# Layer borders of a hybrid decoder trunk: packed column sums, a smaller root and reciprocal, and loads issued by another queue

## The chip, the cores and the metric

The kernel runs on 1 core of one Trainium2 chip. The metric is the device time of one execution in microseconds, the median of the runs.

## What is computed

A trunk of 4 layers over 1024 prompt tokens and 8 single-token samples, with 1024 features. All is float32. Layers 0 and 3 are of kind a (gated MLP with spatial mixing), layer 1 is of kind b (sliding-window attention with rotary embedding), layer 2 of kind c (a convolution and a gated linear recurrence):

```python
def rms_norm(x, g):
    y = xf * lax.rsqrt(jnp.mean(xf * xf, axis=-1, keepdims=True) + NORM_EPS)
    return (y * g.astype(jnp.float32)).astype(x.dtype)

for i in range(DEPTH):
    hp = rms_norm(xp, norm_pre[i])
    yp = mixer(hp)                       # a, b, c, a; ends in a product with w_out
    xp = xp + rms_norm(yp, norm_post[i])
```

The mean of squares is over the features. So at each border between two layers two norms follow one another: the post norm of the layer that ends (its output must be known for all features of a token) and the pre norm of the layer that begins.

## The kernel before

Tokens lie along the columns (1032 = 3 chunks of 344) and features along the 128 partitions, in 8 tiles (KT). A weight unit is 128 x 1024 values, which make one output tile of 128 features for all tokens. SP loads units into a ring of three (`weights`, L373), ScalarE rounds one to its high part (`w_high`, L848), VectorE subtracts for the low part (`w_low`, L1313), and TensorE adds three products (high by high, high by low, low by high) of 344 columns for each of the 8 feature tiles: 24 products for a chunk, 72 for a unit. Each engine runs its own program, written out by hand; the order in it is fixed, and a wait on a semaphore holds all that stands behind it on that engine or queue.

The border is `cross(prev, L)` on ScalarE and VectorE, `last_pair` and `first_pair` on TensorE. The last two output tiles of a layer are computed chunk by chunk: pieces (0,0), (1,0), (0,1), (1,1), (0,2), (1,2), where the first number is the tile and the second the chunk (L456). `post(L, c)` sums the squares of the outputs over the partitions with two matmuls against a matrix of ones (L490, L491, 128 x 128 by 128 x 344 in plain float32, each two instructions in the trace). The second one reads `rx`, where ScalarE has put the squares of the second tile. ScalarE takes the root of all 344 columns from bank 6 into `rx` (`root_post`, L873), and VectorE its reciprocal (`inverse`, L1341). Then `tiles(c, ks)` runs on VectorE over the 8 feature tiles of the chunk: for two tiles at a time the product with `rx` (L1355), for each the addition to `x` (L1358), and once ScalarE has made the high part `h_hi` (L889) the low part `h_lo` (L1335). ScalarE also squares each new tile of x (L894) into a ring of six, and TensorE sums these squares over the partitions (`square_sum`, L531) between the products of the next layer's first two units (L520). The root of that sum is `root_pre` (L879). The pre norm is applied to the results only, when VectorE reads them (`first_reads`, L1375, and `read`, L1425), which frees their banks. In layers of kind a VectorE must also add the outputs to a first half (`out_add`, L1322) before they are squared.

In `first_pair` the unit 0 of chunk 0 comes first, then unit 1 of chunk 0, then the post sum of chunk 2, then both units of chunk 1 and of chunk 2. The sum of chunk 1 uses bank 6 and waits for the root of the post sum of chunk 2, which stands on ScalarE behind six tiles of chunk 1. Units 2 and 3 follow (`unit_by_parts`). SP stores x after the tiles of each chunk (L397), behind the load of weight 2, so that its place can be used by the layer; weight 3 is issued when the first pair has ended.

Each layer then starts on ScalarE with waits for the stored x and the last low part, and DMAs for its constants: the spatial weights in a (L967 to L971), cosine, sine, mask and sinks in b (L1079 to L1085), the states in c (L1190, L1191). In layer b VectorE waits for all seven loads, then signals that the key is read. ScalarE issues the key's swap of halves for the rotary embedding (four DMAs, L1092), VectorE rotates (L1574 to L1577), ScalarE copies the key (L1100) and issues four output DMAs (L1102 to L1105), and after these the first query's swap. `rotate_q` and the low part of weight 4 stand behind that swap on VectorE. In layer c VectorE computes the decay constants (L1768 to L1791, tiny operations) before the first of eight convolutions (`conv`, L1800 on); the low part of weight 4 stands behind the third.

## Time and profile before

| | us |
|---|---|
| median of 3 runs | 2553.09 (2552.48 to 2553.47) |
| the profiled execution | 2552.86 |
| its span in the trace | 2550.8 |
| TensorE busy | 2382.4 |
| VectorE busy | 1280.9 |
| ScalarE busy | 899.9 |

Times in the rows are microseconds from the span's start unless a row says ns. PE is TensorE, DVE is VectorE, ACT is ScalarE; ACTq and SPq are the queues on which they issue. L12 is line 12 of the kernel. Matmuls are pipelined: the duration of one is about twice the distance to the next. A number in brackets at the end of a row is the idle time before it and what ended it.

### The profile page before, as it was taken

The page shows a single profiled execution, that of the slowest core. Times are in us where ns is not written, and L with a number is a line of the kernel's source. Part 1 is how long each engine was busy: PE and PEld are TensorE (multiplying, and loading weights), DVE is VectorE, ACT ScalarE, POOL GpSimd, SP SyncE. Part 2 cuts the span into 40 slices and gives each one's busy share as a digit, 9 for nine tenths or more (in the row PEclk, how much of TensorE's full clock was granted, in tenths as well). Part 3 has the DMA queues.
Part 4 walks back from the last instruction along what each step waited for, and adds up shares of the span by engine and source line. Part 5 has one row for each costly group of instructions (what it writes and reads, how often), then busy time and mean ns, then how long its engine had stood idle before and what let it go on. Part 6 is the DMA issues. An engine that isn't in the chain of part 4 may idle for free.

```text
span 2550.8 us, 34906 instructions
## 1 busy us (share of the span) xinstructions
PE 2382.4 (93%) x14951; PEld 2295.4 (90%) x14951; DVE 1280.9 (50%) x1769; ACT 899.9 (35%) x1242; POOL 92.9 (4%) x44
## 2 busy tenths in 40 slices
PE   8999999998999869997988989899999999998995
PEld 7998999998999868885988989889998999998995
DVE  4443454545334746665268566456443454545236
ACT  5223223233223325455342356344223323234221
POOL 0000000000000002222000001000000000000000
PEclk9999999999999989998999999999999999999998
DMA  3111111111122421110321111313111111111122
GB/s 128 42 50 42 38 41 47 41 44 34 42 84 65 131 61 51 42 50 26 108 70 58 50 41 34 111 55 95 42 50 34 43 42 44 42 46 35 42 91 93
DMA packets 58490, 145.80 MB, mean 57 GB/s; under 512 B 8904, under 2 KB 29528, under 8 KB 58328
## 3 DMA queue, kind: packets, MB, share of 16 engines
q1 hardware_dynamic: 41936, 116.57, 15.0%
q10 hardware_dynamic: 16400, 27.00, 3.4%
q8 instruction: 118, 1.93, 0.3%
q14 instruction: 36, 0.29, 0.0%
HBM read 121.47 MB, written 18.37 MB: 55 GB/s over the span
## 4 chain that ended last, share of the span: by engine, by line
PE 77%; DVE 10%; ACT 5%; DVEq 2%; DMA 2%; ACTq 2%; issue 1%
PE ps L440 58%; PE ps L664 5%; PE ps L520 3%; PE ps L583 2%; PE ps L531 2%; PE ps L811 1%; DVE w_lo L1313 1%; PE ps L456 1%; PE ps L576 1%; PE ps L706 1%; PE ps L681 1%; DVE x L1358 1%; PE ps L692 1%; DVE l_y_lo L1537 1%; DVE l_acc L1355 1%
## 5 line engine op out<-in xcount | busy, mean ns | idle before, releaser
L440 PE MATMUL ps<-l_h_hi,w_hi 128*128 128x344 f32 x2448 | 529.2, 325 | 39.4 <-DVE w_lo L1313 36.1
L440 PE MATMUL ps<-l_h_lo,w_hi 128*128 128x344 f32 x2448 | 523.0, 322 | 0.0
L440 PE MATMUL ps<-l_h_hi,w_lo 128*128 128x344 f32 x2448 | 519.5, 321 | 0.0
L440 PEld LDWEIGHTS ps<-l_h_hi,w_hi 128*128 128x128 f32 x2448 | 412.3, 190 | 44.0 <-DVE w_lo L1313 38.0
L440 PEld LDWEIGHTS ps<-l_h_lo,w_hi 128*128 128x128 f32 x2448 | 416.8, 190 | 0.0
L440 PEld LDWEIGHTS ps<-l_h_hi,w_lo 128*128 128x128 f32 x2448 | 410.8, 189 | 0.0
L1313 DVE TENSOR_TENSOR w_lo<-w_raw,w_hi 128x1024 fp32r<-128x1024 f32 x182 | 222.6, 1223 | 223.5 <-ACT w_hi L848 203.5
L1425 DVE TENSOR_TENSOR l_tmp<-ps,rx 128x1032 f32<-128x1032 f32 x64 | 78.9, 1233 | 323.9 <-PE ps L440 323.9
L848 ACT ACTIVATE w_hi<-w_raw 128x1024 fp32r<-128x1024 f32 x182 | 190.6, 1047 | 105.7 <-DMA w_raw<-in_wu 65.3
L440 PE MATMUL ps<-l_y_hi,w_hi 128*128 128x344 f32 x912 | 197.5, 325 | 32.4 <-ACT l_y_hi L1036 19.7
L440 PE MATMUL ps<-l_y_hi,w_lo 128*128 128x344 f32 x912 | 193.8, 321 | 0.0
L440 PEld LDWEIGHTS ps<-l_y_hi,w_hi 128*128 128x128 f32 x912 | 154.4, 190 | 36.3 <-issue 16.3
L440 PE MATMUL ps<-l_y_lo,w_hi 128*128 128x344 f32 x804 | 171.9, 322 | 0.0
L440 PEld LDWEIGHTS ps<-l_y_hi,w_lo 128*128 128x128 f32 x912 | 153.3, 189 | 0.0
L992 ACT ACTIVATE l_tmp<-l_tmp 128x1032 f32<-128x1032 f32 x32 | 34.1, 1067 | 304.5 <-DVEq L1466 304.5
L440 PEld LDWEIGHTS ps<-l_y_lo,w_hi 128*128 128x128 f32 x804 | 137.2, 191 | 0.0
L997 ACT ACTIVATE l_tmp<-l_tmp 128x1032 f32<-128x1032 f32 x32 | 34.1, 1067 | 262.8 <-DVEq L1471 262.8
L415 POOL TENSOR_TENSOR l_sc<-l_sc,l_rq 128x1024 f32<-128x1024 f32 x32 | 71.3, 2227 | 1144.5 <-DVE l_rq L1645 1144.5
L976 ACT ACTIVATE l_v<-l_v 128x1032 f32<-128x1032 f32 x32 | 34.1, 1067 | 217.2 <-DVEq L1447 217.2
L1420 DVE TENSOR_TENSOR ssq<-ssq,sqt 128x1032 f32<-128x1032 f32 x50 | 61.7, 1233 | 92.4 <-ACT sqt L959 75.8
L520 PE MATMUL ps<-l_h_hi,w_hi 128*128 128x344 f32 x192 | 89.9, 468 | 9.3 <-DVE w_lo L1313 9.3
L1140 ACT ACTIVATE l_sc<-l_sc,l_mx 128x256 f32<-128x256 f32 x128 | 63.5, 497 | 92.8 <-DVEq L1638 92.8
(242 smaller groups left out, 3617.9 us busy)
## 6 DMA issues: line engine op xcount, KB each, us to landing
w_raw<-in_wu SPq DMA_DIRECT2D x182, 512.0 KB, 3.6
x_save<-x SPq DMA_DIRECT2D x9, 1376.0 KB, 5.5
x<-x_save ACTq DMA_DIRECT2D x24, 516.0 KB, 6.5
x<-in_xt ACTq DMA_DIRECT2D x8, 516.0 KB, 5.8
l_sw<-l_q ACTq DMA_DIRECT2D x32, 129.0 KB, 3.0
out_y<-x SPq DMA_DIRECT2D x6, 688.0 KB, 3.5
x<-in_xt SPq DMA_DIRECT2D x4, 688.0 KB, 10.5
x<-in_xt SPq DMA_DIRECT2D x4, 344.0 KB, 6.2
```

The costliest lines, as they stand in the source:

```text
L415: nc.gpsimd.tensor_tensor(L.sc[:, i % 2], L.sc[:, i % 2], L.rq[:, i % 2].rearrange("p (h o) -> p h o", o=1).to_broadcast([P, 4, 2 * WIN]), ...
L440: mm = nc.tensor.matmul(ps[:, 3 * slot + ch, 0:CW], wt[:, w, k, :], mv[:, k, ch * CW:(ch + 1) * CW], start=(k == 0 and t == 0), stop=(k == ...
L520: mm = nc.tensor.matmul(ps[:, 3 * j + c, 0:CW], wt[:, (u + j) % W_RING, k, :], mv[:, k, part(c)], start=(k == 0 and t == 0), stop=(k == KT ...
L531: mm = nc.tensor.matmul(ps[:, 7 - c % 2, 0:CW], ones[:, :], square_place(c, k), start=(k == 0), stop=(k == KT - 1))
L583: mm = nc.tensor.matmul(ps[:, 6 + b // 4, (b % 4) * P:(b % 4 + 1) * P], vt[:, b, :], L.ws[:, g, :], start=True, stop=True)
L664: mm = nc.tensor.matmul(ps[:, p % 2, 0:CW], wt[:, w % W_RING, k, :], mv[:, k, part(ch)], start=(k == 0 and t == 0), stop=(k == KT - 1 and ...
L848: nc.scalar.activation(w_hi[:, u % W_RING], w_raw[:, u % W_RING], ACT.Copy).then_inc(w_hi_done, 1)
L976: nc.scalar.activation(tile_of(L.v, m), tile_of(L.v, m), ACT.Gelu_apprx_tanh)
L1140: nc.scalar.activation(L.sc[:, p, h, :], L.sc[:, p, h, :], ACT.Exp, bias=L.mx[:, p, 1, h:h + 1], accum_out=L.mx[:, p, 2, h:h + 1])
L1313: V.tensor_tensor(w_lo[:, u % W_RING], w_raw[:, u % W_RING], w_hi[:, u % W_RING], ALU.subtract).then_inc(w_lo_done, 1)
L1420: V.tensor_tensor(total[:], total[:], part, ALU.add)
L1425: V.tensor_tensor(chunks(out), psum_result(slot), chunks(rx[:]), ALU.mult)
```

## The change

Sums over the partitions are made in four groups of 32 output rows. Group g sums columns 86g to 86g + 85 of the chunk, so that the sum of 344 columns stands in 128 partitions by 86 columns (every partition of a group holds the same values). Root and reciprocal work on these 86 columns (`rs`). VectorE then multiplies the 86 columns by a selector `gsel` (1 where the partition is in group g) into 344 columns of `rx`, TensorE multiplies that by the ones (`spread`), which brings each group's values to all partitions, and ScalarE copies the result from the bank to `rx`. The root takes no scale 1/D any more and its bias is 1e-6 D: the spread adds up 32 equal values, and 32 is the root of D = 1024. On TensorE the sums and spreads stand inside pieces (after some k) where the post sum stood behind them. The root of chunk 2 moves ahead of the tiles of chunk 1. The layers' loads go from ScalarE to SP, behind the load of weight 3; the outputs of layer b too. In layer b the signals that key and value are read come first, VectorE waits for two of the loads only, and the key's copies stand behind the high part of weight 4. In layer c the decay constants stand behind the third convolution.

```diff
             for L, prev in zip(layers, [None] + layers):
...
+                    if u == L.u0 + 3:
+                        if prev is not None:
+                            sp.wait_ge(*L.x_saved.at(16 * CH))
+                        sp.wait_ge(*L.h_done.at(CH * KT))
+                        sp.wait_ge(*L.sq_done.at(CH * KT))
+                        layer_loads(L)
+                    if L.kind == "b" and u == L.u0 + 5:
+                        sp.wait_ge(*L.k_rot.at(1))
...
+                    if L.kind == "b" and u == L.u0 + 8:
+                        sp.wait_ge(*L.vtok_done.at(2))
...
+            def group_sums(bank, src, start=True, stop=True):
+
+                for g in range(G):
+                    mm = nc.tensor.matmul(ps[32 * g:32 * g + 32, bank, 0:GW], ones[:, 0:32],
+                                          src[:, g * GW:(g + 1) * GW], start=start, stop=stop)
+                return mm
+
+            def spread(bank, c):
+
+                return nc.tensor.matmul(ps[:, bank, 0:CW], ones[:, :], rx[:, part(c)], start=True, stop=True)
+
+            def post_sums(L, c):
+
                 pe.wait_ge(*L.yssq_done.at(LAST + c + 1))
                 pe.wait_ge(*L.ysq_done.at(LAST + 2 * c + 2))
-                nc.tensor.matmul(ps[:, 6, 0:CW], ones[:, :], ssq[:, part(c)], start=True, stop=False)
-                nc.tensor.matmul(ps[:, 6, 0:CW], ones[:, :], rx[:, part(c)], start=False, stop=True).then_inc(L.yssq_mm.sem, 1)
+                if c:
+                    pe.wait_ge(*L.rp_set.at(c))
+                group_sums(6, ssq[:, part(c)], stop=False)
+                group_sums(6, rx[:, part(c)], start=False).then_inc(L.yssq_mm.sem, 1)
+
+            def post_spread(L, c):
+
+                pe.wait_ge(*L.yinverse.at(c + 1))
+                spread(6, c).then_inc(L.yspread.sem, 1)
+
+            def pre_spread(L, c):
+
+                pe.wait_ge(*L.inverse.at(c + 1))
+                spread(7 - c % 2, c).then_inc(L.spread.sem, 1)
...
+                def sums_inside(c):
+
+                    return lambda k: post_sums(L, c) if k == 2 else post_spread(L, c) if k == KT - 1 else None
 
                 piece(0, 0)
                 piece(1, 0)
-                piece(0, 1)
-                post(L, 0)
+                piece(0, 1, sums_inside(0))
                 piece(1, 1)
-                piece(0, 2)
-                post(L, 1)
+                piece(0, 2, sums_inside(1))
                 piece(1, 2)
...
                             square_sum(k, 0)
+                            if k == 2 and prev is not None:
+                                post_sums(prev, 2)
...
+                            if k == 5 and prev is not None:
+                                post_spread(prev, 2)
...
                             square_sum(k, c)
+                            if k == 6:
+                                pre_spread(L, c - 1)
+                unit_by_parts(u + 2, r + 2, L.h_hi, L.h_lo, lambda k: pre_spread(L, 2) if k == 4 else None)
```

ScalarE and VectorE in the border:

```diff
                     out_squares(1, 0)
+                    root_post(0)
                     out_squares(0, 1)
-                    root_post(0)
+                    rp_copy(0)
...
                         tiles(0, range(2, 5))
+                    root_post(1)
                     out_squares(0, 2)
...
-                    root_post(1)
+                    rp_copy(1)
...
                         w_high(L.u0 + 1)
+                    root_post(2)
+                    if L is not None:
+                        tiles(1, range(0, 2))
+                    rp_copy(2)
...
                     w_high(L.u0 + 2)
-                    tiles(2, range(0, 6))
+                    tiles(2, range(0, 2))
+                    rx_copy(0)
+                    tiles(2, range(2, 6))
                     root_pre(1)
                     tiles(2, range(6, KT))
+                    rx_copy(1)
                     root_pre(2)
                     w_high(L.u0 + 3)
+                    rx_copy(2)
...
+                def inverse(place, c, signal):
+
+                    V.reciprocal(rs[:, place, :], rs[:, place, :])
+                    V.drain()
+                    V.tensor_tensor(in_groups(rx[:, part(c)]), rs[:, place, :].rearrange("p (o n) -> p o n", o=1).to_broadcast([P, G, GW]),
+                                    gsel[:].rearrange("p (g o) -> p g o", o=1).to_broadcast([P, G, GW]), ALU.mult).then_inc(signal.sem, 1)
...
                         out_add(0, 1)
+                    inverse_post(0)
                     out_sum(1)
...
-                    tiles(0, range(5, KT))
+                    tiles(0, range(5, 6))
+                    inverse_post(1)
+                    tiles(0, range(6, KT))
...
+                if prev is not None and L is None:
+                    tiles(1, range(KT))
+                    inverse_post(2)
+                    tiles(2, range(KT))
+                elif L is not None:
+                    if prev is not None:
+                        inverse_post(2)
+                    tiles(1, range(0, 6))
+                    inverse_pre(0)
+                    tiles(1, range(6, KT))
+                    w_low(L.u0 + 2)
+                    tiles(2, range(0, 4))
                     first_reads(0)
-                    w_low(L.u0 + 2)
-                tiles(2, range(KT))
-                if L is not None:
+                    tiles(2, range(4, 6))
+                    inverse_pre(1)
+                    tiles(2, range(6, KT))
                     first_reads(1)
+                    inverse_pre(2)
+                    w_low(L.u0 + 3)
                     first_reads(2)
-                    w_low(L.u0 + 3)
```

## Rows read from the trace of the kernel before

**Rows 1.** The page: busy time of TensorE, granted clock in 40 slices.
```profile
PE 2382.4 (93%) x14951; PEld 2295.4 (90%) x14951; DVE 1280.9 (50%) x1769; ACT 899.9 (35%) x1242; POOL 92.9 (4%) x44
...
PEclk9999999999999989998999999999999999999998
```

**Rows 2.** The waits of TensorE: total, how often, the longest.
```profile
PE ps L440 <- DVE w_lo L1313: 44.4, 10, 17.4
...
PE ps L531 <- ACT rx L873: 15.6, 3, 5.8
```

**Rows 3.** Timeline of TensorE where it had been idle: start, duration, line.
```profile
847.48 1.49 PE L531 MATMUL ps<-sq_ring,ones 128*128 128x344 f32 x2 [5.80 <-ACT rx L873]
...
914.87 1.23 PE L440 MATMUL ps<-l_h_hi,w_hi 128*128 128x344 f32 x3 [17.43 <-DVE w_lo L1313]
...
1388.44 1.23 PE L440 MATMUL ps<-l_h_hi,w_hi 128*128 128x344 f32 x3 [9.82 <-DVE w_lo L1313]
```

**Rows 4.** The chain that ended last, border a to b.
```profile
803.79 7.88 PE ps L456 x48
...
814.18 0.56 ACT rx L873
...
872.89 3.71 DMA w_raw<-in_wu
```

**Rows 5.** TensorE: a unit (chain), sums (timeline), the 32-column form (groups, its line).
```profile
267.80 11.36 PE ps L440 x72
...
827.73 0.74 PE L531 MATMUL ps<-sq_ring,ones 128*128 128x344 f32 x2
...
828.77 0.74 PE L531 MATMUL ps<-sq_ring,ones 128*128 128x344 f32 x2
...
L725 PE MATMUL ps<-l_kc,l_qz 128*32 128x129 f32 x16 | 0.6, 279 | 0.0
...
  issue: 0.4, 1
```

**Rows 6.** VectorE's groups: busy us, mean ns of one, idle time before.
```profile
L1341 DVE RECIPROCAL rx<-rx 128x344 f32<-128x344 f32 x24 | 55.2, 2299 | 16.5 <-ACT rx L879 10.1 <-ACT rx L873 6.1 <-issue 0.2
...
L1645 DVE RECIPROCAL l_rq<-l_rq 128x4 f32<-128x4 f32 x32 | 5.7, 178 | 2.4
...
L1375 DVE TENSOR_TENSOR l_v<-ps,rx 128x344 f32<-128x344 f32 x12 | 5.6, 511 | 0.5
```

**Rows 7.** Timeline of VectorE, tiles of chunk 1, border a to b.
```profile
837.83 0.88 DVE L1355 TENSOR_TENSOR l_acc<-l_acc,rx 128x688 f32<-128x688 f32 x1
...
840.51 0.87 DVE L1355 TENSOR_TENSOR l_acc<-l_acc,rx 128x688 f32<-128x688 f32 x1
...
843.41 0.87 DVE L1355 TENSOR_TENSOR l_acc<-l_acc,rx 128x688 f32<-128x688 f32 x1
```

**Rows 8.** The chain at the end of layer 0's first pair.
```profile
46.74 3.71 DMA w_raw<-in_wu
```

**Rows 9.** The chain at the start of layer b; landing of the swaps (DMA issues).
```profile
880.53 3.57 DMA l_dx<-in_dx
...
886.15 5.15 DMA l_sw<-l_kf
...
903.71 5.99 DMA l_sw<-l_q
...
913.59 1.24 DVE w_lo L1313
...
l_sw<-l_q ACTq DMA_DIRECT2D x32, 129.0 KB, 3.0
```

**Rows 10.** Timeline of VectorE at the start of layer c.
```profile
1362.02 0.17 DVE L1768 TENSOR_SCALAR l_sp<-l_sp 128x8 f32<-128x8 f32 x1 [0.92 <-ACT l_sp L1196]
...
1368.11 0.09 DVE L1793 MEMSET l_xr<- 128x3 f32 x2
...
1387.16 1.23 DVE L1313 TENSOR_TENSOR w_lo<-w_raw,w_hi 128x1024 fp32r<-128x1024 f32 x1
```

**Rows 11.** Timeline of VectorE in the last border: chunk 2 starts.
```profile
2538.52 0.88 DVE L1355 TENSOR_TENSOR l_acc<-l_acc,rx 128x688 f32<-128x688 f32 x1
```

More of the change, by code:

```diff
@@ L1124, in unit_end @@
                     w_high(L.u0 + j + 2)
-                for m in range(2):
-                    q_swap(2 + m, m)
-                    w_high(L.u0 + 4 + m)
+                q_swap(2, 0)
+                w_high(L.u0 + 4)
+                act.wait_ge(*L.k_rot.at(1))
+                for kv in range(2):
+                    for half in range(2):
+                        nc.scalar.activation(L.kd[64 * half:64 * half + 64, kv, P:P + NT], L.kf[64 * kv:64 * kv + 64, :], ACT.Copy)
+                nc.scalar.drain().then_inc(L.kset.sem, 1)
+                q_swap(3, 1)
+                w_high(L.u0 + 5)
                 for m in range(2):
@@ new lines, in decay_constants @@
+                    V.drain()
+                    V.tensor_tensor(L.sp[:, 3], L.sp[:, 2], L.sp[:, 2], ALU.mult)
+                    V.memset(L.sp[:, 4], 1.0 / 17)
+                    V.drain()
+                    for d in (15, 13, 11, 9, 7, 5, 3, 1):
+                        V.tensor_tensor(L.sp[:, 4], L.sp[:, 4], L.sp[:, 3], ALU.mult)
+                        V.drain()
+                        V.tensor_scalar(L.sp[:, 4], L.sp[:, 4], 1.0 / d, None, ALU.add)
+                        V.drain()
```

204 lines of the change are left out of this document (102 added, 102 removed).

## The prediction

> **What bounds the kernel now.** I read the page first: TensorE is busy in 93% of the span, at the full clock in all but three of 40 slices [rows 1]. So a change away from TensorE can only give back TensorE's idle time, and a change on TensorE only counts where nothing else is late. The waits of TensorE tell where that is [rows 2]: 44.4 us of its idle time end with the low part of a weight (L1313), 15.6 us with the post-norm root (L873) that frees bank 6. The timeline of TensorE gives the places [rows 3]: 5.8 us in the border a to b, 17.43 us at the start of layer b, 9.82 us at the start of layer c; the other two borders that a layer follows make up the rest of the 15.6, 4.9 each. Everything the change touches lies in five stretches: the first pair of layer 0, three borders with the layer start behind each, and the last border. I call T0 the end of a first pair; it is where SP may issue the fourth weight, 872.9 in the border a to b [rows 4].
>
> **Unit prices.** One f32r product of 344 columns takes 11.36/72 = 0.158 us, a piece of 24 takes 3.79 [rows 5]. A column sum in f32 follows three products; two of them stand 1.04 apart, so a sum costs 1.04 - 0.47 = 0.57 us on TensorE [rows 5]. There are 96 of these and 24 in the post sums, 69 us in all. The new sum is 4 matmuls, 8 instructions of 86 columns in four 32-column groups. The nearest row is the sample scores, 16 instructions of 129 columns in 32-column groups, busy 0.6 us in all while each takes 0.279 [rows 5]: they overlap. Half the instructions, half the time: 0.3 us. Bounds: 0.15 (if columns count, not instructions) to 0.57 (no overlap). I take 0.3, since the form is the same. A post sum becomes 0.6 + 0.57 for the spread, as before 2 x 0.57.
> The Trainium skill (TensorE: Matmul & The Clock Gate, Part 3) says that matmuls in different column groups span little more than one of them; by it the sum would be near the low bound, and layer 0 would gain some 3 us more.
> A reciprocal costs 2.30 us for 344 columns and 0.178 for 4 [rows 6], so 6.2 ns a column and 0.69 for 86. With the product by the selector (0.51, as the reads of 344 columns at L1375) and the drain an inverse is 1.25 us instead of 2.35 on VectorE. But it is followed by spread (0.57) and ScalarE's copy (0.56, as the root it replaces [rows 4]), so its latency is about 2.5. Two tiles cost VectorE 843.41 - 840.51 = 2.90 us, 1.45 each [rows 7]. TensorE needs per tile in chunks 1 and 2 six products and a sum: 0.95 + 0.57 = 1.52 now, 1.25 after. So in the borders TensorE bounds now only just, and VectorE does after: the 0.27 saved a tile is mostly not to be had.
>
> **Layer 0.** No tiles of a previous layer: VectorE and ScalarE run ahead, TensorE is the bound from 8.5 to T0, near 47 [rows 8]. Saved: 24 x 0.27 = 6.5; added: 2 spreads inside, 1.1; 5.4. The loads of the layer go out from SP while ScalarE is in the root, so 0.7 us of idle before the fifth unit goes too. Gain 6; 3 us more or 7 less by the bounds of the sum.
>
> **Border a to b, step by step.** The piece of the second output tile starts at 803.79 [rows 4]. Piece (0,1) with its sums ends at 803.79 + 2 x 3.79 + 0.6 = 812.0. VectorE adds it (0.2 latency, 0.51 as the reads) to 812.7, inverts to 814.0; TensorE, which waits for that in order, spreads to 814.5 (idle 2). Tiles of chunk 0 start at 815.3. The order on VectorE is then two tiles, add, three tiles, add, sum, one tile: about 826.7, then the inverse, 828.0. TensorE ended piece (0,2) at 814.5 + 7.6 + 0.6 = 822.7 and stands at the spread for 5.3 us: **a new stall**, because the spread is put into TensorE's order right behind the piece, while its inverse is queued on VectorE behind six tiles and three additions. Queued behind the spread is piece (1,2). After 5.8 us of idle the products came at 1.2 GHz for a while (1.49 us for two instructions, [rows 3], where 0.74 is usual, [rows 5]), so I add 1.7 us: the piece ends at 828.6 + 3.8 + 1.7 = 834.1. Its addition, square, the high and the low of weight 1 (0.75 + 0.5 + 1.05 + 1.25) end at 837.6, the third inverse at 838.9, and tiles of chunk 1 start there; now they start at 837.83 [rows 7]. So 1.1 us are lost up to here. From there to T0 it takes 35.0 us now. After, on VectorE: 16 tiles 23.2, three extra drains and lows 1.7, two inverses 2.5, a low of a weight with a wait 2.3, a pair of reads 0.95, waits for ScalarE 0.8, and TensorE's last tile with the spread before it 1.5: 32.9. Net T0 is 1 us earlier.
>
> **Start of layer b.** Now the layer's seven loads are issued by ScalarE behind its last high; they land at 884.1 and only then VectorE lets the key's swap go (landed 891.3), rotates, and ScalarE copies the key and issues four outputs before the query's swap: landed 909.7, low at 913.6 to 914.8 [rows 9]. That is T0 + 42.0, with TensorE out of work since T0 + 24.6. After: reads of the first pair end at T0 + 6.5 (the same content as now, one inverse shorter, but the third copy stands behind the high of weight 3, which must load first). The key's swap is issued there at once. It shares the DMA engines with sine, cosine and mask that SP issues once x is saved (5.5 us after the last tile, T0 + 4), so I give it 8 us instead of the 7.1 it took: T0 + 14.5. Rotation 3.7, query read 1.3: T0 + 19.5. The query's swap then takes 6.5 (now 7.9 behind four outputs in its own queue; with them in SP's queue, in flight together; the later swaps land 3.0 after their issue, which would make 5.5, [rows 9]): T0 + 26. Rotation and low 5.0: T0 + 31. TensorE idle 6.6 us instead of 17.4. Gain 10.8, bounds 8 and 14. The key's copies, now behind the high of weight 4, end by T0 + 28, ahead of the second query's swap. SP's waits for key and value stand before weights that are not due yet. Nothing else becomes late before the attention steps.
>
> **Border b to c.** The same chain without the additions: stalls at the spreads about 1 and 3.9 us, tiles of chunk 1 1.2 us earlier, T0 2.7 earlier if the clock holds, and I take off half of 1.7: 1.9.
> **Start of layer c.** Now 6.1 us of tiny steps (decay constants) stand before the first convolution [rows 10]. They move behind the third, whose low starts TensorE. But the convolution then waits for the states, which SP issues after x is saved: T0 + 4.5, with two issues and their landing near T0 + 8.4, where VectorE is free at T0 + 6.5. Three convolutions with the low take 1388.4 - 1368.1 = 20.3 us now, one waiting 0.4 [rows 10], so 19.9: the low ends at T0 + 28.3, now at T0 + 33.5. The constants then delay the next low: 28.3 + 6.1 + 8.3 (one convolution with its read and low) = T0 + 42.7, where TensorE is done at 28.3 + 13.1 = 41.4 (the unit after the stall at its slow start); now it gets there at 46.6. So 5.2 are gained and 1.3 given back: 3.9.
> **Border c to a.** As b to c, 1.9. The spatial weights land about T0 + 10 as now, so the start gains nothing.
>
> **The last border.** No weights and no next layer, the end is VectorE's tiles. Chunk 0 starts 2 us earlier, but the additions are fed by pieces that TensorE holds back at the spreads: piece (1,2) begins near 2524.4 (now 2519.4) and ends at 2528.1, 2529.8 on the slow clock. Tiles of chunk 1, now at 2528.2, start at 2529 to 2530.7. The last inverse stands behind them and its spread and copy are bare: 1.25 + 1.15 + 0.65, where now a reciprocal of 2.35 stands before 2538.52 [rows 11]. A **loss** of 1.3 to 3.0; I take 2.8.
>
> **Sum.** 6 + 1 + 10.8 + 1.9 + 3.9 + 1.9 - 2.8 = 22.7, on the profiled execution of 2552.86 us (span 2550.8, 2.06 around it); the median of the runs is 2553.09, so 2553.1 - 22.7 = 2530.4, about 2530.
>
> **Rivals.**
> (1) *Sums that don't pack.* If changing from full columns to groups of 32 and back costs the array time, each of the 96 pays it. The idle time before the sample scores ("issue", 0.4 us, once, [rows 5]) is the most the trace allows. A sum is then 0.7: layer 0 loses 4 instead of gaining 6, and TensorE's tile of 1.65 is the bound again, 16 x 0.2 + 2 in each of three borders, 15 in all. Left: 22.7 - 10 - 15 = -2, 2555; half of it gives 2543. For it: the switch there and back comes with each of 96 sums, where the 32-column form now stands once. Against: the overlap in the row. The Trainium skill (TensorEngine Tiling, Key Properties) states that changing the tiling mode drains the array, which speaks for this one. Chance 0.13, spread over 2541 to 2555.
> (2) *The swaps stay slow.* DMA engines are busy when both are issued; if they take the times of now after the loads, TensorE still waits 12 us at layer b: 2536 to 2541. Chance 0.12.
> (3) **Slower**: TensorE now works 1.25 of each 1.45 us in chunks 1 and 2 and stands at every spread. If the granted clock falls there to 1.2 GHz, a tile is 1.9 + 0.6 = 2.5 us, above VectorE's 1.45: 16 x 1 us in each of three borders, 48 us against 22.7: 2578. It decides from the first fall inside chunk 1 that is not lifted. Against: the row of the granted clock is below 9 only at the start of layer b, at the end of its attention and in the last slice [rows 1], each with long idle times. Chance 0.05.
> (4) *Better*: the clock holds at the spreads (1.7 + 0.8 + 0.8 + 1.5), the query's swap takes 5.5 (1.0) and the sum is at its low bound (3): 8.8 more, 2522; with the key's swap at its time of now, 2521. Chance 0.1.
> The forecast itself, 2524 to 2537, has 0.6.
>
> **How the numbers follow.** 0.2% is 5 us, about what a measurement of this kernel can tell from no change. Faster by more needs under 2548: the forecast, (2), (4) and most of (1), 0.9; within 0.2% 0.05 from (1); slower 0.05 from (3) and the end of (1). The range takes in (4) and most of (1) and (2): 2517 to 2545.
>
> **What would show it.** Sums of 8 instructions about 0.3 apart; TensorE idle of 4 to 5 us before the second spread of every border with a low clock behind it; the wait at L531 for the root gone; the idle time of 17.4 at about 6.6 and that of 9.8 at about 5 with a new one of 1 to 2 us one unit later; VectorE without gaps from chunk 1 to T0; the last tile later than now. The prediction is wrong in kind if idle time at the spreads exceeds 6 us, or the swaps land as late after T0 as now.

## The result, and the profile after

The changed kernel takes **2561.38 us** in the median (2552.72 to 2567.59) where the kernel before takes 2553.11 (2549.92 to 2558.83) in the same sessions, 20 runs each. The ratio is 1.0023, interval 1.0014 to 1.0032, so it is about 6 us slower. I had forecast 2530 and a range of 2517 to 2545: wrong in sign. Every ratio below is a kernel's time over that of the kernel before, taken side by side with it, with its 95% interval; "by the ratios" means the difference of two ratios times 2553 us. The profiled execution after took 2557.93 us (span 2555.7).

The page after, as [rows 1]: TensorE is busy 12.6 us longer, part of it at the lower clock, and the slow slices stand in other places.

```profile
PE 2395.0 (94%) x15719; PEld 2285.6 (89%) x15719; DVE 1254.8 (49%) x1793; ACT 903.4 (35%) x1266; POOL 92.5 (4%) x44
...
PEclk9999999999999999998999999999999999999998
```

The waits of TensorE after, as [rows 2] (total, how often, the longest). The 44.4 us for the low of a weight are 26.1; the 15.6 for the post-norm root are gone; in their place stand 29.0 us at a spread (L545).

```profile
PE ps L545 <- DVE rx L1409: 29.0, 7, 8.3
PE ps L489 <- DVE w_lo L1380: 26.1, 9, 6.1
```

The timeline of TensorE after, as [rows 3]: the two spreads of the last pair in the border a to b, the start of layer b, the start of layer c with its new second wait, and the bare spread of the last border.

```profile
815.23 1.19 PE L545 MATMUL ps<-rx,ones 128*128 128x344 f32 x2 [2.11 <-DVE rx L1409]
...
830.99 0.94 PE L545 MATMUL ps<-rx,ones 128*128 128x344 f32 x1 [5.18 <-DVE rx L1409]
...
911.63 0.65 PE L489 MATMUL ps<-l_h_hi,w_hi 128*128 128x344 f32 x1 [5.29 <-DVE w_lo L1380]
...
1383.89 0.43 PE L489 MATMUL ps<-l_h_hi,w_hi 128*128 128x344 f32 x1 [2.84 <-DVE w_lo L1380]
...
1398.51 0.43 PE L489 MATMUL ps<-l_h_hi,w_hi 128*128 128x344 f32 x1 [2.99 <-DVE w_lo L1380]
...
2542.06 0.94 PE L545 MATMUL ps<-rx,ones 128*128 128x344 f32 x1 [8.28 <-DVE rx L1409]
```

To see where time went I took the end of the low part of the same weights (VectorE's timeline, the 64th, 68th, 69th and so on of 182) in both traces, and the change in length of each stretch between them. The last four columns are kernels of the experiments below. All are profiled executions, one for each kernel, in us; minus is shorter than before. (For border c to a the stretch runs on to the sixth weight of the layer.)

| stretch | forecast | changed | loads_only | sums_only | spread_behind | by_border_pairs |
|---|---|---|---|---|---|---|
| start to border a to b | -6 | +0.8 | -1.4 | -1.5 | -4.0 | -5.2 |
| border a to b | -1 | **+7.5** | +0.1 | +7.3 | +1.6 | -2.2 |
| start of b | -10.8 | **-11.6** | -8.3 | +0.3 | -11.5 | -11.1 |
| rest of b | 0 | +2.3 | +4.4 | +1.5 | +3.9 | +5.0 |
| border b to c | -1.9 | **+2.8** | +0.1 | +2.4 | -3.2 | -4.1 |
| start of c | -3.9 | -3.5 | -4.4 | +0.7 | -3.5 | -3.5 |
| rest of c | 0 | -0.2 | -0.2 | +0.2 | -1.8 | -0.2 |
| border c to a | -1.9 | **+2.0** | -0.8 | +4.4 | -3.1 | -2.9 |
| layer a | 0 | +1.2 | +1.2 | +1.1 | -0.3 | +0.9 |
| last border | +2.8 | +3.5 | -0.7 | +5.6 | +0.9 | -4.2 |
| sum | -22.7 | +4.9 | -9.9 | +22.1 | -21.0 | -27.5 |

The starts of b and c came as forecast. Layer 0 and the borders did not.

### The profile page after: what moved, and what is told of

It reads as the page before. It is cut to its first block, busy times and chain, and to the rows that moved or that the text cites. A ratio compares the mean times of both kernels' runs of the same rounds, so it can differ in the third digit from the quotient of the medians.

```text
span 2555.7 us, 36511 instructions
## 1 busy us (share of the span) xinstructions
PE 2395.0 (94%) x15719; PEld 2285.6 (89%) x15719; DVE 1254.8 (49%) x1793; ACT 903.4 (35%) x1266; POOL 92.5 (4%) x44
## 4 chain that ended last, share of the span: by engine, by line
PE 80%; DVE 9%; ACT 4%; DVEq 2%; ACTq 1%; DMA 1%; issue 1%
PE ps L489 58%; PE ps L743 5%; PE ps L505 4%; PE ps L595 3%; PE ps L662 2%; PE ps L890 2%; PE ps L655 1%; PE ps L785 1%; DVE w_lo L1380 1%; PE ps L760 1%; PE ps L771 1%; DVE x L1436 1%; DVEq L1435 1%; PE ps L539 1%; PE ps L796 1%
## 5 line engine op out<-in xcount | busy, mean ns | idle before, releaser
L1512 DVE TENSOR_TENSOR ssq<-ssq,sqt 128x1032 f32<-128x1032 f32 x50 | 61.7, 1234 | 91.7 <-ACT sqt L1058 75.5
```

The lines of the kernel that those rows point to most:

```text
L1512: V.tensor_tensor(total[:], total[:], part, ALU.add)
```

## The experiments

### The halves of the change

loads_only is the kernel before with the second half of the change: the loads and outputs on SP, the key's swap first, the decay constants later. sums_only has the first half alone. Their edits are hunks of the diff shown above; the core of each:

```diff
 loads_only
-                act.dma_start(L.cos[:], io["cos"]).then_inc(L.rope_in.sem, 16)
+                    sp.dma_start(L.cos[:], io["cos"]).then_inc(L.rope_in.sem, 16)
...
 sums_only
-                    mm = nc.tensor.matmul(ps[:, 7 - c % 2, 0:CW], ones[:, :], square_place(c, k), start=(k == 0), stop=(k == KT - 1))
+                    mm = group_sums(7 - c % 2, square_place(c, k), start=(k == 0), stop=(k == KT - 1))
```

> The kernel before with the second half of the change alone: SP issues the layers' loads, the key's swap goes first, the key's outputs go out through SP, the decay constants stand behind the third convolution; sums, roots and reciprocals stay as they were. Theory A (the loss of the changed kernel lies in the sums' half, in the borders): the idle time at the start of layer b falls from 17.4 to about 5.5 us (11.7 gained) and that of layer c from 9.8 to about 5.8 in two pieces (4 gained), about 2 are given back in the attention: 2539 us. Theory B (the loads through SP delay weights, and the swaps are only fast because the border before them ended late): both starts gain 5 together or less, 2548 us or more. Every T0 (end of a first pair) stays where it was by both.

> The kernel before with the first half of the change alone: the packed sums, the root and the reciprocal on 86 columns, the spreading product and the copy. Theory A: it keeps all the losses of the changed kernel (T0 of the border a to b 8 us later than before, T0 of layer 0 about 1 later, the last border 3.5 longer) and loses the gains of 13 to 14 us at the starts of b and c: about 2573 us. Theory B (the loads' half costs as much as it gains): about 2560 us, as the changed kernel.

Measured: loads_only 2541.27 (2533.54 to 2542.72, 6 runs), ratio 0.9942 [0.9926, 0.9957]; sums_only 2573.03 (2572.31 to 2580.34, 5 runs), ratio 1.0081 [1.0067, 1.0096]; before 2552.42. By the ratios -14.8 and +20.7, which add up to the +5.9 of the whole change. **The whole loss lies in the sums' half**, theory A. The traced execution of loads_only took 2542.72 us, where two of the six took 2533.5 and 2533.8, so its stretches add up to 9.9 us gained and not to 14.8. In loads_only TensorE stands 9.16 us at the start of b instead of 17.43, and T0 stays (the border is 0.1 longer):

```profile
905.26 1.23 PE L478 MATMUL ps<-l_h_hi,w_hi 128*128 128x344 f32 x3 [9.16 <-DVE w_lo L1319]
```

It gave 8.3 us there and not the 11.7 expected, and 4.4 of them went again in the rest of b, at the same work. The windows show how (stretch, its length, busy time of each engine, granted clock); first before, then loads_only, the same products:

```profile
915.00:972.00 57.00, 54.70 (x348) 50.46 (x349) 25.97 (x69) 21.32 (x49) 6.93 (x4) 0.97 0.19 49
```
```profile
905.00:966.00 61.00, 58.12 (x346) 53.42 (x347) 26.01 (x70) 21.30 (x49) 6.64 (x4) 0.90 0.17 45
```

The granted clock is 0.90 instead of 0.97, and the same products keep TensorE busy for 58.12 us instead of 54.70. In both kernels the clock is at its lower level (0.50) from 905 to 910 us. Before, TensorE is idle there, where it costs nothing; in loads_only it works (first before, then loads_only):

```profile
905.00:910.00 5.00, 0.00 (x0) 0.00 (x0) 0.28 (x1) 0.79 (x1) 0.00 (x0) 0.50 0.25 79
```
```profile
905.00:910.00 5.00, 4.74 (x16) 4.75 (x17) 1.34 (x2) 0.88 (x1) 0.00 (x0) 0.50 0.43 97
```

### The spread in front of the held piece

```diff
-                    return lambda k: post_sums(L, c) if k == 2 else post_spread(L, c) if k == KT - 1 else None
+                    return lambda k: post_sums(L, c) if k == 2 else post_spread(L, c) if k == KT - 1 and c == 0 else None
...
                 piece(1, 2)
+                post_spread(L, 1)
```

> The changed kernel with the spreading product of chunk 1 (post-norm) moved behind the last piece of the last pair, instead of ahead of it: TensorE runs piece (1,2) while VectorE is at the inverse. Theory A (the piece that is held behind the spread makes the last addition, the square, and through the ring of six squares ScalarE late, so that chunk 1 starts at 844.8 instead of about 839 in the border a to b): about 5 us come back in the border a to b, 1 to 3 in each of the other three, 2549 us. Theory C (the loss is the price and the clock of the packed sums): within 2 us of the changed kernel.

Measured: 2536.68 (2531.61 to 2538.17, 5 runs), ratio **0.9929** [0.9916, 0.9942]: 24 us below the changed kernel by the ratios, twice what theory A asked for, from one matmul in each of the four borders that stands one piece later. Not all of the 24 us is the move. In the traces the borders are 5.9, 6.0, 5.1 and 2.6 us shorter than in the changed kernel, 19.6 in all; 4.8 more lie in the stretch up to the first border, where the two kernels have the same code. What the held piece did shows on ScalarE and VectorE of the changed kernel in the border a to b (ScalarE first):

```profile
838.78 0.49 ACT L985 ACTIVATE sq_ring<-x 128x344 f32<-128x344 f32 x1 [5.30 <-PE ps L539]
...
841.37 1.06 ACT L929 ACTIVATE w_hi<-w_raw 128x1024 fp32r<-128x1024 f32 x1
```
```profile
839.77 0.58 DVE L1402 SCALAR_TENSOR_TENSOR l_h_lo<-x,g_pre,l_h_hi 128x344 fp32r<-128x344 f32 x1 [5.69 <-ACT l_h_hi L980]
...
842.46 1.23 DVE L1380 TENSOR_TENSOR w_lo<-w_raw,w_hi 128x1024 fp32r<-128x1024 f32 x1 [1.68 <-ACT w_hi L929]
...
844.80 0.87 DVE L1433 TENSOR_TENSOR l_acc<-l_acc,rx 128x688 f32<-128x688 f32 x1
```

ScalarE waits 5.30 us for a place in the ring of six squares, since the sum that frees it stands on TensorE behind the held piece; behind that wait on ScalarE stand the high part of tile 7 (VectorE waits 5.69 for it), the last square and the high part of the weight. Chunk 1 starts at 844.80. In spread_behind TensorE waits 1.38 us at that spread, ScalarE's square comes without a wait, and chunk 1 starts at 834.23, on a trace that is 4.8 us ahead at the border's start (so 5.8 us earlier in its own time):

```profile
826.18 0.56 PE L545 MATMUL ps<-rx,ones 128*128 128x344 f32 x1 [1.38 <-DVE rx L1410]
```
```profile
828.10 0.47 ACT L986 ACTIVATE sq_ring<-x 128x344 f32<-128x344 f32 x1
```
```profile
834.23 0.87 DVE L1434 TENSOR_TENSOR l_acc<-l_acc,rx 128x688 f32<-128x688 f32 x1
```

The windows of TensorE split a border into the last pair from its second unit on (first of each two rows) and the first pair up to T0 (second). Border b to c before, after, and in spread_behind:

```profile
1289.00:1311.00 22.00, 21.67 (x129) 20.62 (x130) 12.29 (x18) 10.05 (x21) 0.00 (x0) 1.00 0.09 25
1311.00:1355.00 44.00, 39.11 (x194) 33.31 (x193) 40.37 (x58) 22.51 (x46) 0.00 (x0) 0.92 0.30 103
```
```profile
1288.00:1316.00 28.00, 24.11 (x158) 22.46 (x159) 16.03 (x27) 12.37 (x27) 0.00 (x0) 0.88 0.07 20
1316.00:1357.00 41.00, 37.00 (x350) 26.92 (x348) 30.73 (x52) 20.91 (x45) 0.00 (x0) 1.00 0.32 107
```
```profile
1279.00:1300.00 21.00, 20.92 (x154) 19.74 (x154) 13.16 (x23) 11.47 (x25) 0.00 (x0) 1.00 0.08 26
1300.00:1343.00 43.00, 38.70 (x361) 28.07 (x362) 34.33 (x58) 21.96 (x48) 0.00 (x0) 1.00 0.31 108
```

The last pair went from 22 to 28 us: 3.9 of stall, and 24.11 us of busy time instead of 21.67 for the same pieces, at a clock of 0.88. The first pair went from 44 to 41. With the spread behind, the last pair is back at 21 and the first pair stays near 42. So the first pair gave back 3 us of the 6 that the stall took. The same split in the border a to b, the last pair before and then both rows after:

```profile
803.00:826.00 23.00, 21.41 (x127) 20.36 (x128) 14.97 (x22) 9.37 (x17) 0.00 (x0) 1.00 0.23 69
```
```profile
804.00:838.00 34.00, 26.09 (x158) 24.02 (x159) 19.21 (x33) 12.19 (x24) 0.00 (x0) 0.85 0.16 47
838.00:882.00 44.00, 40.16 (x359) 29.38 (x357) 31.71 (x54) 20.77 (x44) 0.00 (x0) 0.92 0.36 121
```

34 and 44 us where the same windows of before are 23 and 47 long. Behind two stalls the pieces keep TensorE busy for 26.09 us at a clock of 0.85, 21.41 before: 4.7 by the clock.

### Which engine holds the first pair

Three kernels free one side each. squares_later and vector_freed start from the changed kernel, root_first from loads_only.

```diff
 squares_later (ScalarE)
-                        tiles(0, range(6, KT))
+                        tiles(0, range(6, KT), squares=False)
                     out_squares(1, 2)
                     if L is not None:
                         w_high(L.u0 + 1)
+                        square(0, 6)
+                        square(0, 7)
...
 vector_freed (ScalarE, then VectorE)
+                        tiles(0, range(6, KT), squares=False)
+                        w_high(L.u0 + 1)
+                        tiles(1, range(0, 4), squares=False)
                     out_squares(1, 2)
...
+                    tiles(1, range(0, 4))
+                    if prev is not None:
+                        if prev.kind == "a":
+                            out_add(1, 2)
+                        inverse_post(2)
...
 root_first (ScalarE)
-                    tiles(1, range(0, 6))
+                    tiles(1, range(0, 2))
                 if prev is not None:
                     root_post(2)
+                if L is not None:
+                    tiles(1, range(2, 6))
```

> The changed kernel with one change on ScalarE: in a border the squares of tiles 6 and 7 of chunk 0 (for the pre-norm) stand behind the last square of the last pair and the high part of the next weight, so that ScalarE no longer waits 5.3 us for a place in the ring of six squares before it comes to these. The spreads stay where the changed kernel has them. Theory R (the ring wait is what makes chunk 1 late): the tiles of chunk 1 start 2 us earlier in the border a to b and T0 comes 2 us earlier in three borders, 4 to 7 us below the changed kernel in all. Theory A' (TensorE is the bound, and the held piece costs it the same): the tiles come 2 us earlier, but T0 moves by under 0.7 us in each border and the kernel stays within 2 us of the changed one.

Measured: 2555.22 (2550.83 to 2565.41, 12 runs), ratio 1.0010 [0.9999, 1.0021], 3.3 us below the changed kernel by the ratios, with intervals that overlap. In its trace, of an execution of 2565.41 us, the border a to b is 2.2 us shorter than in the changed kernel and the two others are not (+0.3 and +1.2): the wait is only renamed there. In the border b to c ScalarE now waits for the held piece at the last square, and VectorE behind it for the high of the weight:

```profile
1320.22 0.46 ACT L944 ACTIVATE rx<-ps 128x344 f32<-128x344 f32 x1 [4.49 <-PE ps L505]
```
```profile
1322.00 1.22 DVE L1387 TENSOR_TENSOR w_lo<-w_raw,w_hi 128x1024 fp32r<-128x1024 f32 x1 [5.48 <-ACT w_hi L929]
```

The ring was the first in line, not the cause.

> The changed kernel with VectorE and ScalarE freed of the piece that is held behind the spread: in a border ScalarE makes the high part of the second weight and of four tiles of chunk 1 ahead of the last square of the last pair, and VectorE the low of the weight and four tiles of chunk 1 ahead of the last addition and the third inverse. The spreads stay where the changed kernel has them, so TensorE still stands 5.2 and 3.9 us. Theory V (the queue of VectorE alone sets T0; what hurts is that its tiles of chunk 1 wait for the held piece): the tiles of chunk 1 start 5 us earlier and T0 comes 4 to 5 us earlier in each of three borders, 12 to 15 us below the changed kernel. Theory B (both engines are within 2 to 3 us of being the bound: from the end of the held piece TensorE itself needs 36.6 us to T0, 144 products of 0.158, 24 sums of 0.48 and the rest, and takes 39 in the border b to c and 43 in the border a to b): T0 comes 1.5 to 2.5 us earlier in the borders b to c and c to a and 3 to 6 in a to b, 6 to 11 us in all. Theory A' (TensorE alone): under 3 us in all.

Measured: 2557.59 (2550.72 to 2562.03, 9 runs), ratio 1.0015 [1.0002, 1.0028], 2.0 us below the changed kernel by the ratios. VectorE starts chunk 1 of the border b to c at 1308.79, 26.2 us behind the start of piece (1,0) at 1282.59, where the changed kernel takes 34.3 (1287.92 to 1322.19). That is 8 us earlier, and yet the border is 3.0 us longer than before, as in the changed kernel (2.8); a to b is 4.6 shorter than there. Of the three theories only A', under 3 us in all, gave this time; V had asked for 12 to 15 and B for 6 to 11. But the run doesn't decide between them, since the edit added a stall of its own. TensorE now stands 2.86 us at the post sums; the profile names no releaser, and the last square, which the sums read, stands on ScalarE behind four tiles and ends 0.1 us before they start. The products behind that stall are slow again, and VectorE, four tiles into chunk 1 by then, waits for two roots of sums that TensorE makes, 1.83 us for the post-norm's and 4.88 for the pre-norm's (0.76 at the same root in the changed kernel). In order: VectorE's first tile, TensorE's sum, ScalarE's last square, VectorE's wait:

```profile
1308.79 0.87 DVE L1443 TENSOR_TENSOR l_acc<-l_acc,rx 128x688 f32<-128x688 f32 x1
```
```profile
1315.36 0.46 PE L539 MATMUL ps<-ssq,ones 128*32 128x86 f32 x5 [2.86 <-issue]
```
```profile
1314.82 0.44 ACT L944 ACTIVATE rx<-ps 128x344 f32<-128x344 f32 x1
```
```profile
1327.49 0.69 DVE L1417 RECIPROCAL rs<-rs 128x86 f32<-128x86 f32 x1 [4.88 <-ACT rs L960]
```

So VectorE's queue alone doesn't set T0 here: it was 8 us early and was stopped by TensorE's sums. A version that frees VectorE with no such wait wasn't tried, and what the stall at the spread costs through VectorE and what through TensorE stays open.

> loads_only (plain sums, reciprocals on 344 columns, as before; loads by SP) with one move: ScalarE's post-norm root of chunk 2 stands behind two tiles of chunk 1 instead of six, so that TensorE doesn't stand 5.8, 4.9 and 4.9 us at the first square sum of chunk 1, for bank 6. Theory A': these 15.6 us are idle time of the engine that bounds the border; until VectorE, some 3.5 us behind in before, becomes the bound, they come out at T0: 2.5 to 3.5 us in each of three borders and 1 to 2 us of slow clock behind the stall; 8 to 14 us below loads_only's 2541: 2527 to 2533. Theory V (VectorE bounds the border): within 2 us of loads_only.

Measured: 2539.86 (2536.66 to 2542.75, 5 runs), ratio 0.9948 [0.9936, 0.9960], where loads_only has 0.9942: nothing, and my theory A' falls. The idle time of 5.81 us at chunk 1 in loads_only became one of 5.77 at chunk 2, 12 us later, where TensorE waits for VectorE's next tile:

```profile
846.00 0.91 PE L569 MATMUL ps<-sq_ring,ones 128*128 128x344 f32 x1 [5.81 <-ACT rx L911]
```
```profile
857.98 0.63 PE L558 MATMUL ps<-l_h_hi,w_hi 128*128 128x344 f32 x1 [5.77 <-ACT l_h_hi L927]
```

Before the change, then, VectorE with its long reciprocals holds the first pair. After it each engine waits for the other within one first pair. In the border b to c of the changed kernel (1320 to 1361 us) TensorE waits 3.7 us for tiles of VectorE and ScalarE, and VectorE waits 1.7 us for roots of TensorE's sums:

```profile
PE ps L595 <- DVE l_h_lo L1402: 2.5, 2, 1.8
PE ps L595 <- ACT l_h_hi L980: 1.2, 1, 1.2
```
```profile
DVE rs L1407 <- ACT rs L960: 1.7, 3, 0.8
```

sums_in_pairs (below) bears that out from TensorE's side, without the stall.

### Price of a packed sum

```diff
 plain_sums
-                for g in range(G):
-                    mm = nc.tensor.matmul(ps[32 * g:32 * g + 32, bank, 0:GW], ones[:, 0:32],
-                                          src[:, g * GW:(g + 1) * GW], start=start, stop=stop)
-                return mm
+                return nc.tensor.matmul(ps[:, bank, 0:CW], ones[:, :], src, start=start, stop=stop)
...
 sums_in_pairs (on spread_behind)
-                            square_sum(k, c)
+                            if k % 2:
+                                square_sum(k - 1, c)
+                                square_sum(k, c)
```

> The changed kernel with each packed sum replaced by one product of 344 columns, as before; the root still takes 86 columns, so the norms are wrong, and everything else waits and runs in the same order. Theory A (the border's order is what costs, a sum costs 0.48 packed and 0.57 plain): layer 0 becomes longer by 24 x 0.09 = 2 us and the whole kernel slower by 2 to 6 us, 2562 to 2566. Theory C (the packing costs more than its place in TensorE's order shows, through the granted clock: in layer 0 the clock came up at 19.9 us instead of 13.9, and it fell in the borders): the clock comes up at 14 us again and the kernel is faster than the changed one by 3 us or more, 2556 or less.

Measured: 2565.40 (2565.08 to 2566.26, 5 runs), ratio 1.0045 [1.0031, 1.0058]: 5.6 us above the changed kernel by the ratios, within theory A. Packing is worth something, and theory C is out.

> spread_behind with the packed sums of the pre-norm taken two at a time (behind every second group of products), 48 changes from full columns to groups of 32 and back instead of 96; the same instructions otherwise. Theory D (a packed sum costs 0.48 us on TensorE in layer 0 where I forecast 0.3, because each change between full columns and groups of 32 costs about 0.2): two sums in a row stand for about 0.76 instead of 0.96, and the kernel becomes 5 to 9 us faster than spread_behind, 2528 to 2532. Theory I (each of the four small products costs its 0.12 wherever it stands): the same time as spread_behind, 2536 to 2538, or up to 2 us slower where a tile's square comes late.

Measured: 2536.29 (2533.26 to 2539.67, 5 runs), ratio 0.9937 [0.9925, 0.9949], the time that theory I gave, but for another reason. In layer 0 the pairs do pay: the low of the sixth weight ends at 72.0 us instead of 75.5 in spread_behind. Of these 3.5 us only 0.7 are left at the first border; 2.8 go between the 21st and the 25th low, where the two kernels have the same code. The price of a change is plain. The timeline of TensorE in chunk 1, first the changed kernel, a sum behind each six products, then in pairs:

```profile
31.63 0.35 PE L539 MATMUL ps<-sq_ring,ones 128*32 128x86 f32 x8
...
33.05 0.36 PE L539 MATMUL ps<-sq_ring,ones 128*32 128x86 f32 x8
```
```profile
30.92 0.36 PE L539 MATMUL ps<-sq_ring,ones 128*32 128x86 f32 x8
31.09 0.33 PE L539 MATMUL ps<-sqt,ones 128*32 128x86 f32 x8
...
33.44 0.50 PE L539 MATMUL ps<-sqt,ones 128*32 128x86 f32 x16
```

One sum: 33.05 - 31.63 - 6 x 0.158 = 0.47 us. Two in a row: 33.44 - 30.92 - 12 x 0.158 = 0.62. So the second costs 0.15, **the packed sum itself costs 0.15 us, and the change to groups of 32 and back 0.32**. That the sums are plain float32 between f32r products isn't the price: in plain_sums one float32 sum of full columns among six products costs 33.19 - 31.67 - 6 x 0.158 = 0.57 us, and one that is followed by the spread, float32 too, costs the same 33.77 - 33.19 = 0.58.

```profile
31.67 0.74 PE L538 MATMUL ps<-sq_ring,ones 128*128 128x344 f32 x2
...
33.19 0.74 PE L538 MATMUL ps<-sq_ring,ones 128*128 128x344 f32 x2
33.77 0.74 PE L542 MATMUL ps<-rx,ones 128*128 128x344 f32 x2
```

In the borders 24 sums in pairs should then save 12 x 0.32 = 3.8 us of TensorE each, and the three borders are 0.4 and 0.1 and 0.6 us shorter than in spread_behind: VectorE is right behind.

The Trainium skill (TensorEngine Tiling, Key Properties) says that a change of the tiling mode drains the array. These rows agree that a change costs time, 0.32 us for both ways; they don't show how much of it is the drain.

### Putting it together

spreads_inside moves three more things; by_border keeps two of them only where a gated layer ends and lets ScalarE's third copy stand two tiles later; by_border_pairs takes the sums of layer 0 in pairs; by_border_plain is by_border with plain sums.

```diff
 spreads_inside (on spread_behind)
-                piece(1, 1)
+                piece(1, 1, lambda k: post_spread(L, 0) if k == 4 else None)
...
-                            if k == 2 and prev is not None:
+                            if k == 4 and prev is not None:
                                 post_sums(prev, 2)
...
 the last border:
-                    tiles(1, range(KT))
+                    tiles(1, range(0, 4))
                     inverse_post(2)
+                    tiles(1, range(4, KT))
...
 by_border
+                if L.kind != "a":
+                    post_spread(L, 0)
+                piece(1, 1, lambda k: post_spread(L, 0) if k == 4 and L.kind == "a" else None)
...
-                        tiles(1, range(0, 2))
+                        tiles(1, range(0, 4))
                     rp_copy(2)
...
 by_border_pairs
+                            elif k % 2:
+                                square_sum(k - 1, c)
+                                square_sum(k, c)
```

> spread_behind with three more moves: the spread of chunk 0 stands inside piece (1,1), behind its fifth group of three products, instead of ahead of it; the sums of chunk 2 (post-norm) stand two groups later in the first pair; in the last border alone the inverse of chunk 2 stands behind four of the eight tiles of chunk 1. Theory A' (TensorE is the bound of a border, from the second unit of the last pair to T0, so every microsecond that it stands at a spread comes out at T0, and the slow clock behind it on top): the 2.1 us at the first spread and the 1.3 us at the sums go in three borders, T0 of each 2 to 4 us earlier; the last border loses its bare inverse, spread and copy, 3 us; together 9 to 13 us below spread_behind's 2536.7: 2524 to 2528. Theory V (VectorE's queue of tiles is the bound of a border, the stalls cost only where they delay its tiles): the borders stay as they are, the last one still gains 3: 2533 to 2535.

Measured: 2534.63 (2528.40 to 2536.34, 5 runs), ratio 0.9922 [0.9911, 0.9934]. Against spread_behind the border a to b is 3.1 us shorter and the last one 5.1, but b to c is 3.5 longer and c to a 3.1. There no additions stand ahead of the inverse, which is ready early, and my spread behind the fifth group came too late for VectorE (first tile of chunk 0 in the border b to c, spread_behind, then spreads_inside):

```profile
1288.61 0.88 DVE L1434 TENSOR_TENSOR l_acc<-l_acc,rx 128x688 f32<-128x688 f32 x1 [0.18 <-ACT rx L972]
```
```profile
1289.39 0.88 DVE L1434 TENSOR_TENSOR l_acc<-l_acc,rx 128x688 f32<-128x688 f32 x1 [2.42 <-ACT rx L972]
```

> spreads_inside with its first two moves only where the layer that ends is a gated one (its last additions are VectorE's, fed by TensorE); the others have the spread of chunk 0 ahead of piece (1,1) and the sums of chunk 2 behind the third group again, as spread_behind; and in every border ScalarE's third copy of the post-norm stands behind four tiles of chunk 1 instead of two. Theory B: the border a to b keeps the 3 us that spreads_inside gained on spread_behind, the other two get back the 3 us each that it lost (its spread stood 2.2 us too late for VectorE), the last border keeps its 5; the 1.5 us that VectorE's low stood behind the copy go in three borders and give 0.5 to 1.5 us each: 2523 to 2528. If the engines' queues are not the reason for the difference: 2533 to 2537, as these two.

Measured: 2528.33 (2525.89 to 2528.76, 4 runs), ratio 0.9905 [0.9891, 0.9918], 0.3 us above the upper end of the expectation. All four borders are now shorter than before (-3.4, -4.1, -2.8, -4.1). The windows of TensorE, border b to c:

```profile
1278.00:1300.00 22.00, 21.47 (x157) 20.19 (x157) 14.14 (x24) 11.92 (x26) 0.00 (x0) 1.00 0.08 25
1300.00:1341.00 41.00, 37.71 (x360) 27.46 (x358) 33.45 (x58) 21.98 (x47) 0.00 (x0) 1.00 0.32 111
```

> by_border with the packed sums of the first layer alone taken two at a time. No border stands before that layer and TensorE is its bound, so 12 changes of array form fewer count there: theory D (a change costs 0.2 us) gives 2 to 3.5 us less than by_border. If the 3.5 us that sums_in_pairs gained in the first layer were the chance of when the clock came up, it gives nothing.

Measured: **2523.80** (2522.09 to 2526.50, 4 runs), ratio 0.9890 [0.9877, 0.9904]: the fastest, 28 us below before and 3.8 below by_border by the ratios. The expectation was 2 to 3.5 below by_border, with a change at 0.2 us. At the low of the sixth weight it is 3.8 us ahead of by_border, which is 12 x 0.32; at the first border it is 4.9 ahead, and the rest, at the same code, I put down to where the clock lay.

> by_border with every packed sum replaced by one product of 344 columns (the root still takes 86 columns, so the norms are wrong). What the packing is worth on TensorE once the stalls are gone: by the durations in TensorE's order 0.48 against 0.57 for 120 sums, of which 24 in the first layer count in full and the 72 of the borders where TensorE is late: 3 to 8 us more than by_border. By the 0.3 of my forecast it would be 10 us or more.

Measured: 2531.02 (2525.17 to 2533.41, 4 runs), ratio 0.9914 [0.9900, 0.9927]. Packing is worth 2.3 us by the ratios, less than what a run varies by, and under the 3 to 8 expected: where VectorE is close behind, TensorE's microseconds do not count in full.

## Why the prediction was wrong, point by point

- **Price of the sum** (unit prices): I took 0.3 us by half the instructions of the sample scores [rows 5]. It is 0.47, of which 0.32 is the change of form; the sample scores pay that once in 16 instructions. I had the mechanism as rival (1), had priced it at 0.4 and given it 0.13. Against the 0.57 of a plain sum 0.1 is saved, not 0.27.
- **Layer 0**, -6 forecast, +0.8 measured: 24 x 0.17 = 4.1 of the difference is that price. The rest is the clock. Six kernels have the code of the changed kernel in this stretch, and they took between -4.0 (spread_behind) and +1.6 (squares_later) against before, -0.7 in the mean; so the forecast less the price, -1.9, is within what one execution can show, and +0.8 alone says little. At 17 us a product still takes 0.49 in the one, where 0.32 is usual, and 0.32 in the other. The row of the changed kernel (timeline of TensorE):

```profile
17.09 0.49 PE L595 MATMUL ps<-l_h_hi,w_lo 128*128 128x344 f32 x1
```

- **Stalls at the spreads**: 2 and 5.3 us forecast in the border a to b, 2.11 and 5.18 measured; 3.9 forecast for b to c and c to a, 3.89 and 3.90 measured. This was read right. For the slow clock behind them I put 1.7 in a to b; it was 4.7, and 2.4 in b to c.
- **That they cost next to nothing**, the step that failed: I let piece (1,2) end at 834.1 and chunk 1 of the border a to b start only 1.1 later than before, then took 32.9 us from there to T0. Chunk 1 started at 844.80, not 838.9: 0.8 from the start of the border, the rest from the clock and from ScalarE's queue, where I had not looked at what stands in front of the high part of the weight (a square that waits for a place in the ring). From 844.80 to T0 at 881.3 it took 36.5 and not 32.9: 1.5 for VectorE behind the third copy, 2.2 for TensorE's end (VectorE waits 3.75 us there, where I had 1.5). By 0.3 a sum TensorE's tile would be 1.25 us against VectorE's 1.45, and it could have caught up 0.2 a tile; at 1.42 it can't. spread_behind shows the stall's part: 5.9, 6.0 and 5.1 us of the three borders, 2.6 of the last. My sign for an error of kind, idle time above 6 us at a spread, asked for the wrong quantity: no stall of the three borders was longer than 5.18.
- **Start of b**: T0 + 31 forecast, 911.63 - 881.3 = T0 + 30.3. The parts were off in both directions (ScalarE's issue of the key's swap and its landing, then the query's swap, against 8 and 6.5):

```profile
888.30 2.56 ACTq L1171 DMA_DIRECT2D l_sw<-l_kf  x4
...
898.15 2.46 ACTq L1171 DMA_DIRECT2D l_sw<-l_q  x4
```
```profile
892.90 1.23 DVE L1669 TENSOR_TENSOR l_sw<-l_sw,l_sin 128x1032 f32<-128x1032 f32 x1 [3.88 <-DMA l_sw<-l_kf]
...
906.49 1.23 DVE L1669 TENSOR_TENSOR l_sw<-l_sw,l_sin 128x1032 f32<-128x1032 f32 x1 [8.49 <-DMA l_sw<-l_q]
```

  4.6 us for the key, 8.3 for the query. Rival (2) came for the query's swap alone, which took 7.9 before; the key's, 7.1 before, made up for it, and TensorE waits 5.29 us and not 12. That the sum came out right is luck in part.
- **Start of c**: 9.82 to 2.84 and 2.99, where I said 5 and 1.3; 3.5 against 3.9 in sum.
- **Last border**: a loss of 2.8 forecast, 3.5 measured; the spread of 8.28 us is bare as forecast. spreads_inside shows what it costs: with the inverse among the tiles of chunk 1 it is 5.1 shorter.
- **Rest of b**, nothing forecast, +2.3: TensorE has as many matmuls there as before (2271) and is busy for 351.56 us instead of 349.71, so most of it is the clock. It isn't lost right behind the shorter idle time as in loads_only: the changed kernel's first 57 us there keep TensorE busy for 54.70 us, as before. Why it falls later stays open.
- **Rival (3)**, slower, had the clock as its mechanism, inside chunks 1 and 2. The clock fell in the last pair instead (0.85 in the border a to b, 1.00 before); in the first pair behind it, it was 0.92, and 0.93 before. Rival and forecast had the same blind spot: which stall is paid, given how much time each engine has left over.

## To carry to other kernels

A stall that a change adds is free only if the engine that stalls has that much slack up to the next point where both meet; take the slack from a window of that engine's busy time, and price the slow clock behind the stall with it. An instruction that waits in order should stand behind the work that needs nothing, not in front of it: one matmul moved behind 24 others, in each of four borders, was worth about 20 us here. When an operation changes the form of the array, count the changes and not the instructions, and take such operations in a row where the array is the bound (in layer 0 here; in the borders it gave 0.1 to 0.6 us each).

## What I had not expected of the hardware

A change from full columns to groups of 32 and back cost 0.32 us of TensorE, twice the packed sum of 344 columns itself (0.15). And equal programs spread with the granted clock: in the stretch up to the first border, the same code in the changed kernel and in spread_behind, they differed by 4.8 us, 3.3 of it within the first 30 us; at 17 us the one still ran products at 0.49 us and the other at 0.32. The 20 runs of the changed kernel differed by 15, the shortest (2552.72) at a mean clock of 0.977 and the longest (2567.59) at 0.972; the clock isn't all of it, since one of 2562.63 had 0.976.
